# Residual sums of seven channel pairs on GpSimd, with VectorE's factor kept in an accumulator bank

## The reference

```python
for i in range(DEPTH):                                   # 2 layers
    op = even_mixer(rmsnorm(x, g_mix_pre[i])) if i % 2 == 0 else cmlp_mixer(rmsnorm(x, g_mix_pre[i]))
    x = x + rmsnorm(op, g_mix_post[i])
    x = x + rmsnorm(ffn(rmsnorm(x, g_ffn_pre[i]), w_ffn_up[i], w_ffn_down[i]), g_ffn_post[i])
```

## Time and profile before

| what | us |
|---|---|
| median of the three runs | 2193.34 |
| lowest and highest | 2193.28, 2195.88 |
| the profiled execution | 2196.57 |
| its span, from the first to the last instruction | 2194.8 |
| TensorE busy | 2161.3 |
| VectorE busy | 1226.8 |
| ScalarE busy | 994.5 |
| GpSimd busy | 202.7 |

### The profile page before, as it was taken

The page is one execution under the profiler, slowest core; times in us unless marked ns, Lnnn a source line. Parts: engine busy times, 40 slices in busy tenths (PEclk is TensorE's granted clock), DMA queues, the critical chain, the costliest instruction groups (busy, mean ns, idle before and its releaser), DMA issues.

```text
span 2194.8 us, 43110 instructions
## 1 busy us (share of the span) xinstructions
PE 2161.3 (98%) x17771; PEld 2141.8 (98%) x17771; DVE 1226.8 (56%) x1330; ACT 994.5 (45%) x1239; POOL 202.7 (9%) x155
## 2 busy tenths in 40 slices
PE   7999999999999999999999999999999999999998
PEld 6999999999999999999989999999999999999998
DVE  6556755754554555455566675575455545545553
ACT  5544544543443344344445564454344334434543
POOL 3001211000000000011213201200000000001112
PEclk9999999999999999999999999999999999999999
DMA  7754454555655665555546555555556565556551
GB/s 221 232 167 145 146 180 153 173 181 183 182 183 183 219 184 179 184 180 181 183 135 191 170 161 182 173 160 176 190 175 188 175 188 176 187 177 187 177 184 62
DMA packets 380643, 386.91 MB, mean 176 GB/s; under 512 B 6804, under 2 KB 378316, under 8 KB 380430
## 3 DMA queue, kind: packets, MB, share of 16 engines
q1 hardware_dynamic: 374530, 380.02, 55.4%
q10 hardware_dynamic: 6036, 5.80, 0.8%
HBM read 380.10 MB, written 5.71 MB: 176 GB/s over the span
## 4 chain that ended last, share of the span: by engine, by line
PE 94%; DVE 4%; ACT 1%; issue 1%; DMA 0%; POOL 0%; SPq 0%; ACTq 0%; DVEq 0%; POOLq 0%
PE ps L1465 30%; PE ps L1467 30%; PE ps L1466 30%; DVE hlo L1048 1%; DVE wlo L1023 1%; PE ps L1485 1%; DVE wlo L1015 1%; PE ps L1487 1%; PE ps L1486 1%; DVE x L1077 0%; PE ps L1770 0%; PE ps L1841 0%; PE ps L1681 0%; PE ps L1667 0%; PE ps L1600 0%
## 5 line engine op out<-in xcount | busy, mean ns | idle before, releaser
L1015 DVE TENSOR_TENSOR wlo<-raw,whi 128x1024 fp32r<-128x1024 f32 x688 | 865.3, 1261 | 764.2 <-ACT whi L605 763.6
L605 ACT ACTIVATE whi<-raw 128x1024 fp32r<-128x1024 f32 x688 | 728.7, 1061 | 1019.4 <-PE ps L1467 1015.2
L1465 PE MATMUL ps<-hhi,whi 128*128 128x264 f32 x2944 | 842.2, 286 | 5.8 <-DVE hlo L1048 3.7
L1467 PE MATMUL ps<-hhi,wlo 128*128 128x264 f32 x2944 | 834.9, 284 | 0.0
L1466 PE MATMUL ps<-hlo,whi 128*128 128x264 f32 x2944 | 834.9, 284 | 0.0
L1465 PE MATMUL ps<-ahi,whi 128*128 128x264 f32 x2560 | 726.6, 284 | 0.0
L1467 PE MATMUL ps<-ahi,wlo 128*128 128x264 f32 x2560 | 724.5, 283 | 0.0
L1466 PE MATMUL ps<-alo,whi 128*128 128x264 f32 x2560 | 724.5, 283 | 0.0
L1465 PEld LDWEIGHTS ps<-hhi,whi 128*128 128x128 f32 x2944 | 555.1, 189 | 12.5 <-issue 6.4
L1467 PEld LDWEIGHTS ps<-hhi,wlo 128*128 128x128 f32 x2944 | 555.1, 189 | 0.0
L1466 PEld LDWEIGHTS ps<-hlo,whi 128*128 128x128 f32 x2944 | 554.8, 188 | 0.1
(11 more groups left out here) (222 smaller groups left out, 1004.6 us busy)
## 6 DMA issues: line engine op xcount, KB each, us to landing
raw<-in_w_ffn_up_dram SPq DMA_DIRECT2D x128, 1024.0 KB, 5.6
raw<-in_w_ffn_down_dram SPq DMA_DIRECT2D x128, 1024.0 KB, 5.3
raw<-in_w_in_even_dram SPq DMA_DIRECT2D x36, 1024.0 KB, 5.2
raw<-in_w_in_cmlp_dram SPq DMA_DIRECT2D x32, 1024.0 KB, 5.5
raw<-in_w_out_even_dram SPq DMA_DIRECT2D x16, 1024.0 KB, 5.4
raw<-in_w_out_cmlp_dram SPq DMA_DIRECT2D x16, 1024.0 KB, 5.3
region<-in_x_prompt_dram SPq DMA_DIRECT2D x4, 512.0 KB, 8.0
out_y_prompt_dram<-region SPq DMA_DIRECT2D x8, 256.0 KB
```

Source lines behind the costliest of these rows:

```text
L605: act.activation(whi[:, QK * q:QK * q + QK, :], raw[:, 2 * par + q // 2, k, :], ACT.Copy).then_inc(w_hi_ready, 1)
L1015: dve.tensor_tensor(wlo[:, QK * q:QK * q + QK, :], raw[:, 2 * par + q // 2, k, :], whi[:, QK * q:QK * q + QK, :].bitcast(F32), ALU.subtrac ...
L1465: pe.matmul(out, whi[:, k, cols], hi[:, k, ::-1], start=(k == 0), stop=False)
L1467: mm = pe.matmul(out, wlo[:, k, cols], hi[:, k, ::-1], start=False, stop=(k == CH - 1))
```

## The change

GpSimd makes the sums of pairs 1 to 7 at k = 0, 1 and 2. The third instruction of `rsqrt` writes the factor to bank 7 (`ps_stat`) in place of `rs_post`, and VectorE's products read it from there. VectorE's order changes with it: `scale` runs one pair further ahead, and follows the low parts.

```diff
@@ residual(k), GpSimd
                 gain(TAIL)
+                for c in range(1, PAIRS if k < 3 else 0):
+                    pool.wait_ge(scaled, (PAIRS - 1) * k + c)
+                    pool.tensor_tensor(x[:, 2 * c:2 * c + 2, :], x[:, 2 * c:2 * c + 2, :], y[:, 2 * c:2 * c + 2, :],
+                                       ALU.add).then_inc(x_added, 1)
@@ rsqrt, VectorE
-                return dve.scalar_tensor_tensor(out=out, in0=out, scalar=1.5, in1=seed, op0=ALU.add, op1=ALU.mult)
+                return dve.scalar_tensor_tensor(out=out if final is None else final, in0=out, scalar=1.5, in1=seed, op0=ALU.add, op1=ALU.mult)
@@ norm_residual, VectorE
-                rsqrt(rs_post[:, :], MIX_POST[k][1], ps_stat, tmp[:, :],
+                rsqrt(rs_post[:, :], MIX_POST[k][1], ps_stat, tmp[:, :], final=ps_stat,
...
-                    dve.tensor_tensor(y[:, 2 * c:2 * c + 2, :], y[:, 2 * c:2 * c + 2, :], twice(rs_post[:, :]), ALU.mult
+                    dve.tensor_tensor(y[:, 2 * c:2 * c + 2, :], y[:, 2 * c:2 * c + 2, :], twice(ps_stat), ALU.mult
                                       ).then_inc(scaled, 1)
-
-                def add(c):
-                    dve.wait_ge(scaled, (PAIRS - 1) * k + c)
-                    dve.tensor_tensor(x[:, 2 * c:2 * c + 2, :], x[:, 2 * c:2 * c + 2, :], y[:, 2 * c:2 * c + 2, :],
-                                      ALU.add).then_inc(x_added, 1)
...
-                    step(dve.tensor_tensor(y[:, t, :], y[:, t, :], rs_post[:, :], ALU.mult))
+                    step(dve.tensor_tensor(y[:, t, :], y[:, t, :], ps_stat, ALU.mult))
...
                 lo_tile(k + 1, 1)
+                scale(2)
                 for c in range(1, PAIRS):
-                    add(c)
                     if c in WAVE_LO_AT:
                         wave_lo(P2, WAVE_LO_AT[c])
-                    if c + 1 < PAIRS:
-                        scale(c + 1)
                     lo_pair(k + 1, c)
+                    if c + 2 < PAIRS:
+                        scale(c + 2)
```

More of the change, by code:

```diff
@@ L1028, in next_lo, with rsqrt @@
                     w_lo(P2 + par, 1 - par, q)
-            def rsqrt(out, st, mean, seed, pre=None, v=None):
+            def rsqrt(out, st, mean, seed, pre=None, v=None, final=None):
                 roots[0] += 1
```

## The result

The changed kernel takes 2198.39 us, the median of ten runs (2197.19 to 2200.73). Ten runs of the kernel before on the same chip have a median of 2195.62 us (2193.28 to 2197.84). The ratio is 1.0018 with a 95% interval of 1.0010 to 1.0026: slower by 3.9 us (2.2 to 5.7). That is little, but it is more than the measurement is uncertain. (The ratio is not that of the medians, which lie 2.8 us apart.) The forecast was 2195.8 us, which is 2.5 us more than the three runs of before, and "within 0.2%". The forecast of 2.5 us lies inside the interval, so the whole time alone can't tell whether it had the right size; the waves can.

A forecast was written before the change was run, and what follows sets the result against it. TensorE, 98% busy, was taken to bound the kernel; lock costs of 0.76 + 0.76 + 0.96 = 2.5 us over three waves, added to the median 2193.34, gave 2195.8 us, range 2191.5 to 2199.5.

The forecast's parts named there:

- the lock: A GpSimd sum, once let in, shuts out VectorE instructions reading two SBUF inputs for 0.99 us; 68% with its wave cost.
- the turn: VectorE's cycle for one pair inside a wave: forecast 3.64 us, against 3.18 before.
- A lock for the whole instruction: The Trainium skill's rule: 1.18 us a turn instead of 0.99, 0.57 us more a wave, total 2197.5 us.
- the bank: Factor in a PSUM bank: products reading it escape the lock; reading costs nothing, writing taken as 0.
- the meeting point: Start of `hlo` of pair 3 on VectorE, after 2.01 us idle; earlier delays are absorbed, later ones count.
- the term: The lock's cost at the end of each wave: 0.76, 0.76 and 0.96 us over the three waves.
- the clock: TensorE's half-clock stretch at wave starts varies between executions; allowed as +-1.5 us on the forecast.
- TensorE's stop at task 5: TensorE's first wait for VectorE in the first wave: to grow from 0.94 to about 1.4 us.
- The stop at task 7: TensorE's second wait in the first wave: to grow, ending at 396.85 instead of 396.09, setting the wave's end, +0.76 us.
- That the lock doesn't reach VectorE's path: Rival, 10%: GpSimd's sums slip into VectorE's products, turn 2.56 us, -1.1 us a wave, 2190.1 us.
- that GpSimd is let in only behind the `hlo` pair: Rival, 8%: the sum shuts out the next `wave_lo` instead; turn about 3.0 us, no change, 2193.3 us.
- That the longer stop lowers the clock: Rival, 5%: TensorE's 1.41 us stop brings a half-clock stretch mid-wave; 2198.3 us with one, 2203.3 with one in each wave.

The follow-up runs named there:

- the memsets: Changed kernel with each GpSimd sum replaced by two memsets that read nothing, same waits and signals: 2191.64 us, ratio 0.9987.
- the kernel with the bank alone: Kernel before with the factor written to bank 7 and read there by VectorE's products, sums still on VectorE: 2195.34 us, ratio 1.0003.
- the clock held up: Useless TensorE matmuls (26, 16, 32) added ahead of the three waves: kernel before 2192.64 us (0.9991), changed kernel 2199.96 us (1.0018).

## Why the prediction was right and wrong

**Right: the lock and the turn.** Forecast against measured: turn 3.64 and 3.61 us; the sum 2.2 and 2.22 us in the second half of a wave, 1.31 where VectorE is idle; the first `hlo` behind `wave_lo` 1.5 and 1.54 us; the products 0.70 and 0.69. The lock costs 1.05 us between starts, where the sum had 0.99 for it and 0.09 for the overlap that is gone. That it is the lock is shown by the memsets (2.56 us a turn). A lock for the whole instruction would have given 1.18 + 0.09 = 1.27 us, which isn't what the trace has.

**Right: the bank.** I took 0, and the kernel with the bank alone moved by 1.0003 (0.9994 to 1.0012). The Trainium skill's other price (VectorE: DVE Perf Modes, the table of the TRN2 errata) would, by the estimate from it, have made a product 0.065 us longer; products from the bank take 0.69 to 0.70 us, those from SBUF 0.70.

**Wrong: what happens at the meeting point.** The step that failed is "*`hlo` of pair 3 stays at 383.83, as the sum of pair 4 runs while VectorE is idle*", and with it "whatever VectorE gained or lost before is absorbed in that 2.01 us". The 2.01 us belong to the execution that was profiled, in which TensorE ran long at half clock. The old order can make use of an earlier end of it, down to 8.2 us into the wave with 0.38 us idle; the new one can't, since its sum of pair 4 runs until 9.7 us into the wave and shuts out an `hlo` of pair 3 that wants to start before (1.55 to 1.84 us for 0.90). Where the meeting point did come late (9.85 us into the third wave) the step held: 18.43 - 17.76 = 0.67 us for the forecast 0.76, three turns of 3.61 - 3.18 = 0.43 us more, less the one sum. Elsewhere it was 1.3 to 1.95. Per wave the term was 0.76 to 0.96; at the granted clocks in the table it is 0.6 to 1.95, and an execution that has some of each comes near the measured 3.9 / 3 = 1.3. That the forecast of 2.5 us in all still lies inside the interval of 2.2 to 5.7 is luck: with the clock held up, where the term stands alone, it is 5.85.

**Wrong in consequence: "the clock" as a mere width.** I carried it as +-1.5 us beside the sum, as if it had nothing to do with the lock. It has: at full clock before gains over a microsecond a wave and after 0.3 at most. A stretch at half clock also costs less than the 2.5 us of its 25 matmuls: the first wave of before gets only 27.62 - 26.01 = 1.6 us shorter without it.

**Wrong: the base and the limit.** The median of three runs, 2193.34, lay at the low end of what ten gave (2195.62); 2.3 of the 2.6 us by which the forecast time is too low come from there. And I took 0.2% for what can't be told from no change and so held my own forecast of 0.1% for "no change"; 0.18% was told, with an interval of 0.10 to 0.26%. The chance for "slower" was therefore too small, with a mechanism in hand that had only one sign.

**Smaller points.** TensorE's stop at task 5 grew to 388.35 - 387.31 = 1.04 us, not 1.41, since TensorE had already stood still for `hlo`, at 386.60 for the last time, and came later to the stop. The stop at task 7, which was to grow as well, shrank from start to start to 394.97 - 394.54 = 0.43 us (0.60 before), for the same reason. It is still the later of the two that sets the end of the wave, as forecast. In the third wave I expected 0.2 us more than in the others because its meeting point is near; this time it was the farthest.

**The rivals.** That the lock doesn't reach VectorE's path, and that GpSimd is let in only behind the `hlo` pair, both fall with the 1.94 us pairs. That the longer stop lowers the clock: the granted clock of after's first wave, 0.94 over 27.92 us, is one stretch of 3.41 us at half clock (0.50) from 373.36 to 376.77 and 1.00 behind it, so the stops of about one microsecond later in it lowered nothing. In that rival I wrote that the clock was low "after starts 3.3 us and more apart". The second wave of before is a nearer case: it begins behind 2.17 us of idle time, and its clock is low too, as its first matmul and its first stretch show:

```profile
1125.53 0.56 PE L1485 MATMUL ps<-hhi,whi 128*128 128x264 f32 x1 [2.17 <-issue]
...
1125.50:1130.50 5.00, 4.97 (x22) 5.00 (x23) 4.63 (x8) 1.81 (x4) 0.00 (x0) 0.50 0.00 0
```

The clock was part of the story in the other direction: it decides how much of the lock shows.

**Still open.** What sets whether a half-clock stretch lasts 3.41 us (first wave of after) or 6.83 us (first wave of before, from 372.72 to 379.55), or isn't there (second wave of the kernel with the bank alone), behind the same idle time. How often each occurs was not measured, so the 3.9 us is explained by its bounds and not as a sum. The three waves of after are together 2.1 us longer than those of before in the profiled executions (84.13 and 82.05), but 3.9 us longer than those of the kernel with the bank alone (80.22).

## What to carry to other kernels

Before an instruction goes from VectorE to GpSimd, look at what VectorE will be running when it arrives: here a sum of 0.62 us became a lock of 1.05 on two-input work. Spared were VectorE's instructions that read a bank, and all of them where GpSimd only wrote. Idle time of an engine that is seen in one execution is no reserve if the engine it waits for was running at half clock then; price a change at full clock as well. To compare two orders of one stretch, hold the clock up in both and compare the stretch: its length then repeats to 0.02 us, while the whole times still scatter by 4 us.

## What the runs showed of the hardware

A sum on GpSimd that waits for a two-input instruction of VectorE goes ahead of VectorE's next one. In each wave of after this happened four times (the sums of 2.22 us), and never was it the other way round. One line's instructions of after (ns min, median, max), the sums and the products:

```profile
L510 POOL TENSOR_TENSOR x<-x,y x21: 1312/2222/2232, 373.1 to 1448.0; 128x528 f32<-128x528 f32 x21
L1076 DVE TENSOR_TENSOR y<-y,ps x21: 687/694/699, 372.4 to 1447.2; 128x528 f32<-128x528 f32 x21
```

The products, with one input in a bank, are never struck: none of 21 is over 699 ns. Here only the product of pair 2 runs beside a sum; with the factor in SBUF it took 1.82 us. Memsets of 0.55 and 0.99 us on GpSimd left `hlo` at 0.90 us a pair.

TensorE's low clock after an idle time of the same length isn't the same from one execution to the next: first waves of 0.90 (before) and 0.94 (the bank alone, after), and second waves of 0.91, 0.94 and 1.00, with the same work ahead of them (but for the place of a factor and a few sums on GpSimd). 16 to 32 matmuls that compute nothing, put into the idle time, kept it at 1.00 in nine waves of nine, and took 1.1 to 1.6 us off each wave of the kernel before.
